# Wider spacing for the rounds of the second recurrence in a planned instruction order

## What is computed

```
h = rmsnorm(x)
q_a, f_a, i_a, g_a, q_b, k_b, v_b, f_b, gates = split(h @ w_in)      # 1024 x 9224
f = lb + (1-lb)*sigmoid(f_a);  k = 1 - f;  q = silu(q_a)             # "hgrn", the second recurrence
S_t = diag(f_t) S_{t-1} + k_t i_t^T;   o_t = S_t^T q_t               # 8 heads of 128 x 128
y_a = (rmsnorm(o) * silu(g_a)) @ w_branch_a
logit[t,s] = q_b.k_b/sqrt(128) + sum_{s<j<=t} log f_b,  s <= t       # "fox", 8 heads of 128
y_b = (softmax(logit) @ v_b) @ w_branch_b
x = x + rmsnorm((gate0*y_a + gate1*y_b) @ w_out)
```

## Time and profile before

| | |
|---|---|
| three runs, median (lowest to highest) | 1213.69 us (1212.59 to 1213.85) |
| the profiled execution's own time | 1211.47 us |
| its span, first to last instruction | 1209.7 us |
| busy: PE, POOL, ACT, DVE | 1154.1, 915.6, 593.3, 458.4 us |
| mean granted TensorE clock | 0.989 |
| POOL's pieces of `wlo` (L2693) | 913, 910.1 us busy, 1030 ns mean |

### The profile page before, as it was taken

The page is one execution under the profiler, slowest core; times in us unless marked ns, Lnnn a source line. Parts: engine busy times, 40 slices in busy tenths (PEclk is TensorE's granted clock), DMA queues, the critical chain, the costliest instruction groups (busy, mean ns, idle before and its releaser), DMA issues.

```text
span 1209.7 us, 21189 instructions
## 1 busy us (share of the span) xinstructions
PE 1154.1 (95%) x8388; PEld 979.5 (81%) x8388; DVE 458.4 (38%) x802; ACT 593.3 (49%) x867; POOL 915.6 (76%) x922
## 2 busy tenths in 40 slices
PE   7999899999899999999999999999999999999997
PEld 7899788777687888788997887887788977888785
DVE  5527655764544111101417566634233133111102
ACT  6364532533555554534554544465556446445533
POOL 4678954431198888798699998779997857888794
PEclk9999999999899999999999999999999999999999
DMA  9887533332175666566465554444766535666563
GB/s 341 276 269 209 140 89 89 117 112 89 32 240 164 191 188 189 180 180 189 120 192 141 141 141 140 123 145 146 230 248 188 157 97 165 191 186 183 169 197 101
DMA packets 182898, 202.10 MB, mean 167 GB/s; under 512 B 7528, under 2 KB 141072, under 8 KB 182032
## 3 DMA queue, kind: packets, MB, share of 16 engines
q1 hardware_dynamic: 177584, 185.78, 51.4%
q10 hardware_dynamic: 5216, 14.97, 3.6%
HBM read 196.51 MB, written 4.21 MB: 166 GB/s over the span
## 4 chain that ended last, share of the span: by engine, by line
PE 67%; POOL 17%; issue 5%; ACT 5%; DVE 5%; DMA 1%; ACTq 0%; DVEq 0%; POOLq 0%
PE ps L724 18%; PE ps L726 17%; PE ps L725 17%; POOL wlo L2693 17%; PE ps L721 12%; PE ps L729 2%; ACT whi L1333 1%; DVE x L1909 1%; DMA raw<-in_w_in 1%; ACT L1333 1%; ACT hThi L1333 0%; DVE red L2364 0%; ACT ps L1333 0%; DVE yg L1901 0%; ACT rl L1333 0%
## 5 line engine op out<-in xcount | busy, mean ns | idle before, releaser
L2693 POOL TENSOR_TENSOR wlo<-raw,whi 128x256 fp32r<-128x256 f32 (+1 forms) x913 | 910.1, 1030 | 278.2 <-ACT whi L1333 276.8
L1333 ACT ACTIVATE whi<-raw 128x1024 fp32r<-128x1024 f32 x324 | 341.1, 1057 | 303.7 <-PE ps L726 277.7
L724 PE MATMUL ps<-whi,hThi 128*128 128x512 f32 (+1 forms) x656 | 262.7, 400 | 8.8 <-POOL wlo L2693 5.3
L726 PE MATMUL ps<-whi,hTlo 128*128 128x512 f32 (+1 forms) x656 | 254.6, 388 | 0.0
L725 PE MATMUL ps<-wlo,hThi 128*128 128x512 f32 (+1 forms) x656 | 254.0, 387 | 0.0
L724 PE MATMUL ps<-hThi,whi 128*128 128x256 f32 x568 | 168.3, 296 | 11.0 <-POOL wlo L2693 3.8
L725 PE MATMUL ps<-hTlo,whi 128*128 128x256 f32 x568 | 163.3, 287 | 0.0
L726 PE MATMUL ps<-hThi,wlo 128*128 128x256 f32 x568 | 162.9, 287 | 0.0
L724 PEld LDWEIGHTS ps<-whi,hThi 128*128 128x128 f32 x656 | 123.3, 188 | 39.2 <-issue 12.1
L726 PEld LDWEIGHTS ps<-whi,hTlo 128*128 128x128 f32 x656 | 123.2, 188 | 26.1
L725 PEld LDWEIGHTS ps<-wlo,hThi 128*128 128x128 f32 x656 | 123.5, 188 | 22.1
(11 more groups left out here) (394 smaller groups left out, 1558.4 us busy)
## 6 DMA issues: line engine op xcount, KB each, us to landing
raw<-in_w_in SPq DMA_DIRECT2D x120, 512.0 KB, 3.7
raw<-in_ffn_w_in SPq DMA_DIRECT2D x176, 256.0 KB, 3.1
raw<-in_ffn_w_down SPq DMA_DIRECT2D x44, 512.0 KB, 4.2
raw<-in_w_mkv SPq DMA_DIRECT2D x16, 512.0 KB, 6.1
raw<-in_ada_w SPq DMA_DIRECT2D x8, 512.0 KB, 6.5
raw<-in_w_o SPq DMA_DIRECT2D x8, 512.0 KB, 4.6
raw<-in_w_branch_a SPq DMA_DIRECT2D x8, 512.0 KB, 3.7
raw<-in_w_branch_b SPq DMA_DIRECT2D x8, 512.0 KB, 3.7
```

What stands on the lines that cost most here:

```text
L724: e.matmul(o, l[0], r[0], start=start, stop=False)
L726: return e.matmul(o, l[1], r[0], start=False, stop=stop)
L1333: return e.activation(o, i, f, **k)
L2693: p = e.tensor_tensor(wlo[c % NHL][:, o], raw[i % NRAW][:, o], whi[c % NHL][:, o], ALU.subtract)
```

## The change

In the table `COST`, the three steps of the fourteen rounds of levels 0 to 6 get other lengths. The numbers are (PE, DVE, ACT) in us.

```diff
     "hgrn": [(0, 6., 2.)] + [(.3, .2, 0)] * 4 
-            + ([(0, 1.8, 1.), (0, 1.4, 0), (.6, .4, 0)] * 2) * 7
+            + ([(0, 2.2, 1.), (0, 2.1, 0), (.6, .5, 0)] * 2) * 7
             + [(0, 1.2, 1.6), (0, 1.2, 0), (.9, .7, 0)] * 2 + ...
```

More of the change, by code:

```diff
@@ L143 @@
     "toh1": [(.5, .7, .6)] * 4, "toh2": [(.5, .7, .6)] * 4,
-    "hgrn": [(0, 6., 2.)] + [(.3, .2, 0)] * 4 + ([(0, 1.8, 1.), (0, 1.4, 0), (.6, .4, 0)] * 2) * 7
+    "hgrn": [(0, 6., 2.)] + [(.3, .2, 0)] * 4 + ([(0, 2.2, 1.), (0, 2.1, 0), (.6, .5, 0)] * 2) * 7
             + [(0, 1.2, 1.6), (0, 1.2, 0), (.9, .7, 0)] * 2 + [(.9, 1.4, 0), (1.8, 1.4, 0), (0, 0, 4.), (0, 1.8, 0), (0, 1.3, 0),
```

## The result

The median after the change is 1218.46 us (nine runs, 1214.72 to 1221.5), against 1212.57 us for the kernel before, timed beside it (nine runs, 1207.54 to 1213.85). The two medians are 5.9 us apart. The ratio of the two kernels is 1.0066, with a 95% interval of 1.0052 to 1.008; by it the change costs 8.0 us (6.3 to 9.7), and this is what I explain. The forecast was slower by 2.9 us.

The account below looks back on a forecast made before the run. POOL's remainders were taken to bound the first part (634 to 752 us), PE the second (752 to 843). Terms -3.6 + 1.7 + 4.8 = +2.9 us on the profiled 1211.47 gave 1214.4, or 1216.6 as median; range 1209.3 to 1220.

Parts of the forecast that it names:

- Term 1: First part, where POOL sets the pace: four pairs of DVE products fewer run against busy POOL, -3.6 us.
- The price: First part: a pair of DVE products of SBUF tensors costs a busy POOL 0.9 us.
- the count of four: First part, up to gt0: 12 steps A and 11 B against a busy POOL instead of 14 and 13, four pairs fewer.
- Term 2: Second part, where PE is the bound: C steps of (5, 1) and (6, 0) now stand there, +1.7 us.
- Term 3: Second part: PE waits where slabs' high parts queue behind steps in ACT; 7.5 less 2.7 of before, +4.8 us.
- Faster: Whole kernel: wider pitch removes the second part's waits, -3.6 + 1.7 - 2.7 = -4.6 us, 1209.1; chance 0.22.
- No change: Second part: PE waits half of that found, 4.6 us, lateness covering one place; sum 0, 1213.7; chance 0.20.
- Nothing moves: Whole kernel: DVE and ACT run ahead and take steps when data are there, so places bind less; 0; chance 0.08.

Follow-up runs that it names:

- (4, 0) behind the eviction of kb3: Changed kernel with step A of round (4, 0) one half earlier, beside kb3.1/0 instead of kb3.1/1; ratio 1.0046 against the kernel before.
- the four repairs: Changed kernel with five steps moved: A of (4, 0) to kb3.1/0, F2 to gt0.2/0, F6 to gt1.2/0, F14 to ga1.1/0, F18 to gt2.1/0; 0.9977 against before.
- the four gaps filled: Changed kernel with unused matmuls on constants ahead of gt1.0/0, ga0.0/0, ga1.3/0 and gt2.2/0, where PE waits; ratio 1.0032 against the kernel before.
- the two mixed kernels: One has the recurrence's steps as in the changed kernel and fox's as before, 1.0049 against the kernel before; the other the reverse, 1.0069.
- F14 apart: Changed kernel with softmax F14 beside ga1.1/0 instead of ga1.0/0, away from step R; ratio 1.0062 against the kernel before.
- these with three more moves: Kernel with the four repairs, with F3 also moved to gt1.0/0 and F15 and F16 to ga1.3/0; ratio 0.9971 against the kernel before.

## Why the prediction was right in its sign and wrong in its size

*Term 1, POOL in the first part: -3.6 forecast, -1.9 measured.* What failed is the claim that moving the steps apart changes only the count of pairs. I followed the queues of ACT and DVE at each place of the second part and at none of the first, because PE's waits there are hidden under POOL. But a wait of ACT for DVE, ahead of `whi`, is a pause of POOL, and POOL is what sets the pace there: POOL's idle time rose by 3.4 us, which the term put at nothing. (4, 0) behind the eviction of kb3 gave back 1.3 of the 1.7 us that are missing; the other 0.4 stay unexplained. The price isn't confirmed either. POOL's busy time fell by 5.3 us, 1.3 for each of four pairs, while shortening ten pairs gave 0.8 each. Some of the pairs that are left now fall into POOL's pauses, as the two products of 0.69 us at 718.85 do, and cost it nothing, so the count of four was too simple. That the first part is 3.2 us shorter than before once the pause is gone, close to the forecast 3.6, comes of a larger gain and an unforeseen loss and is in part luck.

*Term 2, two C steps in the second part: +1.7.* No run measured it by itself. The kernel with the four repairs is in keeping with it: before had 3.6 us of waits from gt0 to gt3.3 and this one 2.1, so with the term its second part would take 93.7 - 3.6 + 2.1 + 1.7 = 93.9 us; it takes 94.4.

*Term 3, the waits: the four places were right and the sizes within 0.6 us, the sum was shaded the wrong way.*

| wait at | forecast | measured |
|---|---|---|
| gt1.0, behind F2 | 2.0 | 2.49 |
| ga0.0, behind F6 | 1.5 | 2.05 |
| ga1.3, behind R and F14 | 2.1 | 2.30 |
| transposes of T | 2.1 | 1.97 |
| ga0.1 and the start of gt0 | 0.7 | 0 |
| sum | 8.4 | 8.8 |

I then took 8.4 down to 7.5, because DVE's products run faster beside an idle POOL. Three of the four waits came out longer than even the undiscounted figure, so the discount had no ground. Less the 3.6 us that PE waited before between gt0 and gt3.3, the term is +5.2; of these 3.6 I had counted 2.7, since my window began at 752 us and ended at 843 and the list leaves out the smallest waits.

*What was missing altogether: the clock.* No term held that a wait costs more than its length. With the four gaps filled the section was 3.0 us shorter and the kernel 4.1 us faster. That is less than 2 x 1.7 = 3.4, since the first stretch cost 1.4 and began while PE still waited. This is the largest of the errors, a term that was put at nothing, and the row for it was in front of me: the first part's granted clock of 0.99 is one such stretch, hidden under POOL there, and I did not ask what it would cost where PE is the bound.

Together: -1.9 + 1.7 + 5.2 + 3.0 = 8.0, against 7.8 in the section and 8.0 in the runs, with the 1.7 of term 2 not measured by itself. The forecast's 2.9 missed 1.7 in term 1, 0.4 in term 3 and 3.0 in the clock. About 0.4 of the sum is counted twice: the wait at ga0.0 was 2.05 us in the three profiles with this place as in after and a half-clock stretch at gt1.0, and 1.70 and 1.66 in the two without one. The sum is then 7.6, and the 0.2 that are left stay open.

*Slips in the working.* They don't change the outcome. The forecast's own range is said to take each wait between half and one and a half of its size. With 7.5 us of waits and 2.7 of before that gives -0.9 to +6.7, 1212.8 to 1220.3, and not 1214.4 to 1219.5. And fox does not keep its start: F0 and F1 stand a half later too, as the lists of the two mixed kernels show.

*The rivals.* "Faster" fell with its condition: the waits were 8.8 us, not under 2. It did describe the kernel with the four repairs, where F2, F6, F14 and F18 no longer stand in front of a slab that PE needs: there term 3 is indeed slightly negative and the kernel wins 2.8 us, of the 4.6 that the rival put on it. "No change" asked for 4.6 us of waits with lateness covering the next place; none of the four covered another, since with those of F2 and F6 gone the other two stayed at 2.30 and 1.97 us. "Nothing moves" was wrong in both parts.

## What to carry to other kernels

When a planner's lengths are made true to the trace, the order it writes still changes only at whole places, and what decides is which long step comes to stand in front of which short one in the in-order queue of a third engine. Follow that queue at every place moved, also where the engine that waits is not the bound, and ask what it feeds. And price a wait of TensorE of about 2 us not at its length alone: a half-clock stretch may follow it, which cost 1.4 to 1.6 us here. Half a slab's delay for two softmaxes was worth 2.1 us of waits, and 5.2 us in the median with the clock.

## What the runs showed of the hardware

A wait in an otherwise dense stream of matmuls can be followed by 3.4 us at 1.2 GHz, and whether it is varies. In the second parts of the profiles of after and of the kernels made here there are eighteen waits of 1.97 to 3.66 us; twelve were followed by such a stretch and six were not. None of the seven waits of 1.35 to 1.83 us was. Of after's waits those of 2.49 and 2.30 us were followed by it, those of 2.05 and 1.97 were not; with the (4, 0) repair alone a wait of 2.51 us at the same place was not; with F14 apart one of 2.05 us before ga0.0 was:

```profile
784.47 0.47 PE L755 MATMUL ps<-whi,hThi 128*128 128x512 f32 x1 [2.05 <-issue]
784.78 0.40 PE L756 MATMUL ps<-wlo,hThi 128*128 128x512 f32 x1
...
785.25 0.62 PE L755 MATMUL ps<-whi,hThi 128*128 128x512 f32 x1
```

This bears on the spread of the changed kernel's times, 6.8 us: the granted clock of its nine executions goes from 0.992 in the fastest to 0.983 in one of the two slowest. It isn't the whole of the spread, since the nine of the kernel before, which has no such wait in its second part, spread over 6.3 us. The kernels whose waits in the second part stayed under 1.1 us (the four repairs, and these with three more moves) show no stretch there in their profiles, nor does the one with filled gaps. The Trainium skill, "TensorE: Matmul & The Clock Gate", section "HAM oscillation — how this bites in real kernels", says that an engine kept waiting for operands between blocks falls back to the lower clock at every block. The trace agrees that such waits bring the lower clock, and not that each does: with waits of about 2 us between blocks of 15 to 35 us it followed some and not others.

Shortening ten pairs of DVE products gave POOL 0.8 us of its own time for each, and the kernel 0.59, because PE was idle for only 2 us in 30 while POOL set the pace.
